# Attention's values product with the values as the stationary side, in three float32r passes, its output already transposed

## What the kernel computes

```python
hcat = jnp.einsum('bsd,de->bse', x, w_in)            # q, k, v of the branches, forget logits, gates
p = jax.nn.softmax(logits, axis=-1)                  # forgetting, block-sparse
o = jnp.einsum('bhqk,bhkd->bhqd', p, v)
# dilated: o and lse per dilation, then
w = jax.nn.softmax(jnp.stack(lses, axis=0), axis=0)
yb = jnp.sum(w[..., None] * jnp.stack(outs, axis=0), axis=0)
merged = sum(gates[:, :, i] * jnp.einsum('bse,ed->bsd', y_i, w_p_i) for i in range(3))
x = layer_norm(alpha * x + jnp.einsum('bsd,de->bse', merged, w_o))
x = layer_norm(alpha * x + swiglu(x))
```

## Time and profile before

| | us |
|---|---|
| runs (3), median | 873.25 (873.02 to 873.25) |
| the profiled execution's own time | 873.52 |
| its span, first to last instruction | 871.7 |
| PE busy | 840.5 (96%) |
| DVE busy | 513.3 (59%) |
| ACT busy | 400.1 (46%) |
| POOL busy | 56.7 (7%) |
| granted TensorE clock, mean | 0.997 |

### The profile page before, as it was taken

The page is one execution under the profiler, slowest core; times in us unless marked ns, Lnnn a source line. Parts: engine busy times, 40 slices in busy tenths (PEclk is TensorE's granted clock), DMA queues, the critical chain, the costliest instruction groups (busy, mean ns, idle before and its releaser), DMA issues.

```text
span 871.7 us, 10732 instructions
## 1 busy us (share of the span) xinstructions
PE 840.5 (96%) x4216; PEld 695.9 (80%) x4216; DVE 513.3 (59%) x728; ACT 400.1 (46%) x536; POOL 56.7 (7%) x86
## 2 busy tenths in 40 slices
PE   3999999999999999999999999999999899999995
PEld 2888888888877888888878889888888688888884
DVE  7565564556796545445685656463778764555436
ACT  3476465543344344444336655554443453344430
POOL 0012331000000000000000324200000000000000
PEclk9999999999999999999999999999999999999998
DMA  9574433457636765664436443435654576656501
GB/s 324 160 257 164 133 119 116 141 181 229 193 104 244 232 194 183 193 203 149 154 108 225 144 159 106 142 103 181 243 177 144 192 246 203 189 183 193 193 0 49
DMA packets 93458, 149.35 MB, mean 171 GB/s; under 512 B 3424, under 2 KB 52832, under 8 KB 93408
## 3 DMA queue, kind: packets, MB, share of 16 engines
q1 hardware_dynamic: 93408, 148.66, 52.5%
HBM read 147.60 MB, written 1.05 MB: 171 GB/s over the span
## 4 chain that ended last, share of the span: by engine, by line
PE 92%; DVE 5%; DMA 1%; ACT 0%; issue 0%; SPq 0%; DVEq 0%
PE bank L1044 82%; PE bank L1059 3%; PE bank L1103 3%; PE bank L1135 2%; DVE w_lo L860 2%; PE bank L1123 1%; PE bank L1069 1%; DMA raw<-in_w_in 1%; DVE stats L977 1%; DVE x L1010 1%; DVE x L974 1%; DVE x L1007 1%; DVE act_lo L865 0%; DVE newton L994 0%; DVE rstd L999 0%
## 5 line engine op out<-in xcount | busy, mean ns | idle before, releaser
L860 DVE TENSOR_TENSOR w_lo<-raw,w_hi 128x2048 fp32r<-128x2048 f32 (+3 forms) x142 | 309.0, 2180 | 91.5 <-ACT w_hi L762 91.0
L1044 PE MATMUL bank<-w_hi,act_hi 128*128 128x512 f32 (+2 forms) x864 | 342.8, 397 | 3.3 <-DVE act_lo L865 3.3
L1044 PE MATMUL bank<-w_hi,act_lo 128*128 128x512 f32 (+2 forms) x864 | 333.3, 386 | 0.0
L1044 PE MATMUL bank<-w_lo,act_hi 128*128 128x512 f32 (+2 forms) x864 | 332.2, 384 | 0.0
L762 ACT CAST w_hi<-raw 128x2048 fp32r<-128x2048 f32 (+3 forms) x142 | 257.2, 1813 | 125.5 <-PE bank L1044 100.4
L1044 PEld LDWEIGHTS bank<-w_hi,act_hi 128*128 128x128 f32 x864 | 163.2, 189 | 33.2 <-DVE act_lo L865 3.7
L1044 PEld LDWEIGHTS bank<-w_hi,act_lo 128*128 128x128 f32 x864 | 162.8, 188 | 33.0
L1044 PEld LDWEIGHTS bank<-w_lo,act_hi 128*128 128x128 f32 x864 | 163.4, 189 | 28.8
L1044 PE MATMUL bank<-w_hi,y_hi 128*128 128x512 f32 x240 | 95.2, 397 | 0.0
L1044 PE MATMUL bank<-w_hi,y_lo 128*128 128x512 f32 x240 | 93.7, 390 | 0.0
L1044 PE MATMUL bank<-w_lo,y_hi 128*128 128x512 f32 x240 | 93.5, 390 | 0.0
(11 more groups left out here) (88 smaller groups left out, 551.3 us busy)
## 6 DMA issues: line engine op xcount, KB each, us to landing
raw<-in_w_in SPq DMA_DIRECT2D x48, 1024.0 KB, 5.2
raw<-in_w_gate SPq DMA_DIRECT2D x44, 512.0 KB, 4.0
raw<-in_w_up SPq DMA_DIRECT2D x44, 512.0 KB, 5.0
raw<-in_w_down SPq DMA_DIRECT2D x22, 1024.0 KB, 4.9
raw<-in_w_o SPq DMA_DIRECT2D x8, 1024.0 KB, 5.2
raw<-in_w_in SPq DMA_DIRECT2D x4, 768.0 KB, 4.4
raw<-in_w_pa SPq DMA_DIRECT2D x4, 768.0 KB, 4.4
raw<-in_w_pc SPq DMA_DIRECT2D x4, 768.0 KB, 4.4
```

The source lines that it names most:

```text
L860: dve.tensor_tensor(weights(w_lo, i, HI_SLOTS), weights(raw, i, RAW_SLOTS), weights(w_hi, i, HI_SLOTS).bitcast(F32), ALU.subtract).then_in ...
L1044: ins = pe.matmul(bank[use[0]][:, 0:width], a, w[:, k, c0:c0 + width], start=start and k == 0 and p == 0, stop=stop and k == nk - 1 and p ...
```

## The change

1. The values are split too: "spread" writes v to `v_hi` (ACT, float32r), DVE makes `v_lo`. There is one buffer for the dilated branch and one that the two other branches share, as now for q and k.
2. A new step "weigh" at half tick k, for unit k-1: DVE takes 1/`denom`. For the forgetting and block-sparse branches DVE also multiplies the probabilities by it in place, one `tensor_scalar` a head. For the dilated branch POOL does that, on the summed probabilities, behind "sum".
3. "turn_p" waits for "weigh", and its result is split: `prob_t_hi` by ACT, `prob_t_lo` by DVE. The buffers hold both tiles of a pair.
4. "values" is done once a pair, after tile 1. The values of the pair (128 columns) are stationary, the transposed probabilities of both heads and tiles move: for key tile 0 512 columns, for key tile 1 256, three passes each. The output has the head's dimension in its rows, and each head's own half of the columns is used (`own_blocks`). ACT and DVE write it straight to `y_hi` and `y_lo`, two operations each on 64 partitions.
5. The transposes of y are gone.

The diff, without the parts that only pass other names or slot lists:

```diff
+Y_SLOTS = [[0, 1, 2], [3, 4], [5, 0, 1]]
...
-                d["pt"] = aux_bank()
+                d["pt"], d["pt_n"] = aux_bank(), count.next("pt")
...
                 stage_of[k]["s2"] = [bank(4), bank(5)]
-                plan.append(("scores2", stage_of[k], g0 + 1))
-            if 0 <= k - 2 < len(units):
+                plan.append(("scores2", stage_of[k]))
+            if 0 <= k - 1 < len(units):
+                plan.append(("weigh", stage_of[k - 1], count.next(("weigh", stage_of[k - 1]["b"] == 1))))
+                stage_of[k - 1]["weigh_n"] = plan[-1][2]
+            if 0 <= k - 2 < len(units) and stage_of[k - 2]["t"] == TT - 1:
                 d = stage_of[k - 2]
                 d["o"] = aux_bank()
-                plan.append(("values", d, g0 + d["b"]))
-                if d["p"] == PAIRS[d["b"]] - 1:
-                    last_y[d["b"], d["t"]] = d["o"]
-                    y_due.append((d["b"], d["t"]))
-
-        y_due = []
-        last_y = {}
+                plan.append(("values", d, count.next("values")))
+                for t in range(TT):
+                    y_turned[d["b"], t] = d["o"]
...
-            for b, t in due:
-                y_turned[b, t] = turn("y", 0, 0, BRANCH_KT[b], t, "y", 3 * ((g0 + b) % 2),
-                                      ("bank", last_y[b, t]))
...
-        values = [sb(f"values{s}", [P, TT, 384]) for s in range(2)]
-        qk_hi = [sb(f"qk_hi{s}", [P, 8, SEQ], F32R) for s in range(2)]
-        qk_lo = [sb(f"qk_lo{s}", [P, 8, SEQ], F32R) for s in range(2)]
+        shapes = [("ac", 384, 6), ("b", 256, 8)]
+        v_hi, v_lo = ([sb(f"v_{part}_{n}", [P, TT, width], F32R) for n, width, _ in shapes] for part in ("hi", "lo"))
+        qk_hi, qk_lo = ([sb(f"qk_{part}_{n}", [P, pairs, SEQ], F32R) for n, _, pairs in shapes]
+                        for part in ("hi", "lo"))
...
-        prob_t = sb("prob_t", [P, 2 * SEQ])
-        y = sb("y", [P, TT, 384])
+        prob_t_hi, prob_t_lo = (sb(f"prob_t_{part}", [P, 3, 2 * P], F32R) for part in ("hi", "lo"))
...
+        def own_blocks(o):
+
+            return [(slice(e * HEAD_DIM, (e + 1) * HEAD_DIM),
+                     o[e * HEAD_DIM:(e + 1) * HEAD_DIM, :].rearrange("p (t e q) -> p t e q", t=TT, e=2)[:, :, e, :])
+                    for e in range(2)]
...
+                elif step[0] == "weigh" and step[1]["b"] == 1:
+                    _, u, n = step
+                    w, pr, s0 = u["w"], both_probs[u["t"]], 2 * (u["u"] % 4)
+                    pool.wait_ge(summed, u["sum_n"])
+                    pool.wait_ge(inverse_done, n)
+                    pool.tensor_tensor(pr[:, :, 0:w], pr[:, :, 0:w],
+                                       rdenom[:, s0:s0 + 2].unsqueeze(2).broadcast_to([P, 2, w]),
+                                       ALU.mult).then_inc(pool_weighed, 1)
...
-                            out = values[(3 * layer + br) % 2][:, t, first:first + width]
+                            out = v_hi[br % 2][:, t, first:first + width]
...
-                    ins.then_inc(drained[b], 1)
+                    ins.then_inc(v_hi_done if v_n else drained[b], 1)
...
-                    act.copy(prob_t[:, 0:2 * u["w"]], bank[b][:, 0:2 * u["w"]]).then_inc(drained[b], 1)
+                    t = u["t"]
+                    act.copy(prob_t_hi[:, t:2 * t + 1, :], group_view(bank[b], t + 1, 2 * P)
+                             ).then_inc(prob_t_hi_done, 1)
+                elif kind == "values":
+                    _, u, _ = step
+                    b, n = u["o"]
+                    act.wait_ge(filled[b], n)
+                    for rows, own_block in own_blocks(bank[b]):
+                        ins = act.copy(hi["y"][rows, Y_SLOTS[u["b"]][u["p"]], :].rearrange("p (t q) -> p t q", t=TT),
+                                       own_block)
+                    ins.then_inc(y_hi_done, 1)
...
+                elif kind == "spread" and step[6]:
+                    _, c, t, (b, n), segs, ev, v_n, _ = step
+                    dve.wait_ge(v_hi_done, v_n)
+                    for what, br, first, col0, width in segs:
+                        if what == "v":
+                            dve.tensor_tensor(v_lo[br % 2][:, t, first:first + width], bank[b][:, col0:col0 + width],
+                                              v_hi[br % 2][:, t, first:first + width].bitcast(F32),
+                                              ALU.subtract).then_inc(drained[b], 1)
...
-                    dve.wait_ge(drained[fb], fn)
+                    dve.wait_ge(v_hi_done, v_n)
...
+                elif kind == "weigh":
+
+                    u = step[1]
+                    s0 = 2 * (u["u"] % 4)
+                    dve.wait_ge(exp_done, 2 * u["u"] + 2)
+                    inverse = dve.reciprocal(rdenom[:, s0:s0 + 2], denom[:, s0:s0 + 2])
+                    if u["b"] == 1:
+                        inverse.then_inc(inverse_done, 1)
+                        continue
+                    link(inverse)
+                    for e in range(2):
+                        pr = prob[u["t"]][e][:, 0:u["w"]]
+                        ins = dve.tensor_scalar(pr, pr, rdenom[:, s0 + e:s0 + e + 1], None, ALU.mult)
+                    ins.then_inc(weighed, 1)
+                elif kind == "turn_p":
+                    u = step[1]
+                    b, n = u["pt"]
+                    t = u["t"]
+                    dve.wait_ge(prob_t_hi_done, u["pt_n"])
+                    dve.tensor_tensor(prob_t_lo[:, t:2 * t + 1, :], group_view(bank[b], t + 1, 2 * P),
+                                      prob_t_hi[:, t:2 * t + 1, :].bitcast(F32),
+                                      ALU.subtract).then_inc(drained[b], 1)
                 elif kind == "values":
-                    u = step[1]
+                    _, u, y_n = step
                     b, n = u["o"]
-                    s0, h0 = 2 * (u["u"] % 4), 2 * u["p"] * HEAD_DIM
-                    dve.wait_ge(filled[b], n)
-                    link(dve.reciprocal(rdenom[:, s0:s0 + 2], denom[:, s0:s0 + 2]))
-                    dve.tensor_tensor(y[:, u["t"], h0:h0 + 2 * HEAD_DIM].rearrange("p (e c) -> p e c", e=2),
-                                      group_view(bank[b], 2, HEAD_DIM),
-                                      rdenom[:, s0:s0 + 2].unsqueeze(2).broadcast_to([P, 2, HEAD_DIM]),
-                                      ALU.mult).then_inc(drained[b], 1)
+                    k = Y_SLOTS[u["b"]][u["p"]]
+                    dve.wait_ge(y_hi_done, y_n)
+                    for rows, own_block in own_blocks(bank[b]):
+                        by_t = [m["y"][rows, k, :].rearrange("p (t q) -> p t q", t=TT) for m in (lo, hi)]
+                        ins = dve.tensor_tensor(by_t[0], own_block, by_t[1].bitcast(F32), ALU.subtract)
+                    ins.then_inc(drained[b], 1)
...
-                    if u["b"] == 1:
-                        pe.wait_ge(summed, u["sum_n"])
-                    else:
-                        pe.wait_ge(exp_done, 2 * u["u"] + 2)
+                    pe.wait_ge(pool_weighed if u["b"] == 1 else weighed, u["weigh_n"])
                     out, done = take(u["pt"])
-                    w = u["w"]
-                    for e in range(2):
-                        for j in range(u["t"] + 1):
-                            ins = pe.transpose(out[:, e * w + j * P:e * w + (j + 1) * P],
-                                               prob[u["t"]][e][:, j * P:(j + 1) * P], ident)
+                    for j in range(u["t"] + 1):
+                        for e in range(2):
+                            c0 = (2 * j + e) * P
+                            ins = pe.transpose(out[:, c0:c0 + P], prob[u["t"]][e][:, j * P:(j + 1) * P], ident)
                     ins.then_inc(done, 1)
...
                 elif kind == "values":
-                    _, u, g = step
+
+                    _, u, _ = step
                     pb_, pn = u["pt"]
                     pe.wait_ge(drained[pb_], pn)
                     out, done = take(u["o"])
-                    w = u["w"]
-                    for e in range(2):
-                        h = 2 * u["p"] + e
-                        for j in range(u["t"] + 1):
-                            ins = pe.matmul(out[:, e * HEAD_DIM:(e + 1) * HEAD_DIM],
-                                            prob_t[:, e * w + j * P:e * w + (j + 1) * P],
-                                            values[g % 2][:, j, h * HEAD_DIM:(h + 1) * HEAD_DIM],
-                                            start=j == 0, stop=j == u["t"])
+                    pair = slice(u["p"] * P, (u["p"] + 1) * P)
+                    for j in range(TT):
+                        cols = slice(j * 2 * P, 4 * P)
+                        for p, (v, pt) in enumerate(((v_hi, prob_t_hi), (v_hi, prob_t_lo), (v_lo, prob_t_hi))):
+                            moving = pt[:, 2 * j:2 + j, :].rearrange("p a q -> p (a q)")
+                            ins = pe.matmul(out[:, cols], v[u["b"] % 2][:, j, pair], moving,
```

(26 more changed lines are left out.)

55 lines of the change are left out of this document (32 added, 23 removed).

## The result

The changed kernel takes 877.34 us (median of 4 runs, 877.08 to 877.74), the kernel before in the same session 873.25 us. The ratio is 1.0045, 95% interval 1.0033 to 1.0058. That is 4.1 us slower. The forecast was 872.4 us, the range ended at 876.2, and "slower" had 0.21. The profiled execution took 877.09 us.

What follows compares the result with a forecast made beforehand. PE was taken to bound the kernel. Per layer, 4.15 us saved against 1.3, 2.0 and 0.4 us of new waits gave -0.45, both layers -0.9, so 872.4 us against 873.25; range 869.4 to 876.2.

Steps and rivals of the forecast that it cites:

- PE's savings: Values product per pair 1.03 instead of 1.35 us, transposes of y gone: 4.15 us a layer, 8.3 together.
- First place: Third scores of unit 7 (dilated first pair, tile 1): PE waits for DVE's reductions behind prob_t_lo; 1.3 us lost a layer.
- Second place: turn_p of unit 7: PE waits for POOL's multiplication, which waits for DVE's reciprocal; 2.0 us lost a layer.
- Third place: Forget gates: two v_lo ahead of f_in on DVE delay cum_row and PE's first scores; 0.4 us lost a layer.
- Elsewhere: Other attention waits stay covered, counted as nothing; unit 11's values product thinly, up to 0.9 us a layer if not.
- DVE's added work: About 15 us more DVE work a layer in attention, most of it falling into DVE's own waits.
- w_lo shuts POOL's multiplication out: Unit 7: DVE's w_lo takes the port first, POOL waits; 875.8 us, 877.6 with unit 11's 0.9 a layer; chance 0.15.
- unit 11's term: Values product of unit 11 waiting for prob_t_lo: up to 0.9 us a layer if its thin cover goes.
- the third rival: Values product: 256-column passes cost as much as long ones, 0.227 us, so 5.4 us comes back; 877.8 us; chance 0.05.
- The first rival: Attention waits are covered better than worked out: 870.5 us, or 865 with no stall and all 8.3 showing; chance 0.30.

Runs made afterwards that it cites:

- Run 2: Changed kernel without DVE's multiplication of the forgetting and block-sparse branches' probabilities by 1/denominator (the reciprocal stays): 876.50 us.
- run 8: Changed kernel with the two v_lo of the third q, k, v product moved behind the forget gates' chain in DVE's queue: 876.16 us.
- run 4: Changed kernel with the values product done half a tick later from unit 7 on, same work: 873.43 us.
- Run 3: Changed kernel with prob_t_lo moved behind the reductions of the same tick in DVE's queue: 874.11 us.
- run 9: Changed kernel with prob_t_lo and dilated reciprocal behind reductions, third product's v_lo behind forget gates, values product half a tick later from unit 7: 866.92 us, again 866.97.
- run 6: Changed kernel with the dilated branch's weighing moved earlier, its reciprocal behind the next unit's reductions: 875.51 us.
- run 5: Changed kernel with the dilated branch's weighing half a tick earlier, right behind the sum and ahead of prob_t_lo: 876.27 us.
- run 7: Changed kernel with DVE instead of POOL weighing the dilated branch's summed probabilities: 876.75 us.
- run 1: Changed kernel without DVE's subtraction that makes prob_t_lo; the buffer holds zeros, PE's passes stay: 870.74 us.

## Why the prediction was wrong

**PE's savings: right within 0.3 us a layer.** The pair costs 1.03 us and y has no transposes. Start to start PE saves about 3.85 us a layer against 4.15 forecast. The difference lies mostly at the first three tile-0 units, whose values product stood next to transposes of q and k: taking it out gave 0.12, 0.41 and 0.39 us there instead of 0.45. PE's busy time fell by 5.7 us where some 8 were forecast. About 2 us of that difference are a low clock in this execution: behind the LayerNorm between the first layer's mixer and FFN (263.8 to 267 us) its product steps took 0.43 us instead of 0.23. Run 2's kernel has the same three groups of waits and no such stretch, and its PE is busy for 832.7 us, 7.8 less than before.

**First place: right in mechanism, at the upper bound in size.** 1.7 us a layer where 1.3 was forecast. It is w_lo, prob_t_lo, reductions, as written. Everything stood later than worked out: the reductions ended at 116.78 and not 115.8, and PE came 0.8 us earlier than before and not 1.4.

**Second place: right.** 1.7 us where 2.0 was forecast. POOL's multiplication took 1.04 us, not the 1.30 of an addition.

**Third place: right in size.** 0.5 and 0.3 us start to start in the two layers, 0.4 forecast; run 8 gives 0.7 of the 0.8 back.

**Elsewhere: this step failed.** "Elsewhere the cover holds ... the values product of unit 11 about 0.2 us after prob_t_lo. That last is thin; if it goes, the price is up to 0.9 us a layer", and the sum took it at nothing. It cost 1.5 us a layer, 3.0 us in all; run 4 confirms it with 3.1. For this place the prediction shows no chain step by step, as it does for the first two. It missed that the displaced reductions move ACT's exponentials, with them w_hi and the w_lo that stands ahead of prob_t_lo. Run 3 shows that link backwards: prob_t_lo moved *behind* the reductions comes earlier at unit 11. Nor had it that turn_p of unit 11 waits for DVE's weighing, 0.17 us a layer.

**DVE's added work** was 17.8 us a layer and not 15. That it was more does not explain the loss: run 9 has nearly all of it.

**The sum.** Set beside each other product step by product step, the two profiled executions give: per layer -3.85, +1.7 +1.7 +1.5, +0.5 or +0.3 at the first scores, and +0.17 at turn_p of unit 11, which is +1.8 and +1.6. Another +0.5 falls outside attention, behind the same LayerNorm, and -0.25 at the start, where the first product came 0.48 us later but the clock rose 1.2 us sooner. Together 3.6 us, as between the spans. The prediction had -0.9 there. Of the 4.5 us between, about 3.0 are unit 11, 0.8 the first place, 0.6 PE's savings, 0.3 turn_p of unit 11, 0.25 what lies outside attention, and the second place gives 0.6 back. The medians are 0.5 us further apart than the profiled executions.

**The rivals.** That w_lo shuts POOL's multiplication out (875.8, 877.6 with unit 11) came nearest in time and did not happen: the multiplication started 0.59 us ahead of w_lo and took 1.04 us. The agreement with 877.6 is chance but for unit 11's term. The lock that the Trainium skill states (page "SBUF — State Buffer", section "Who interferes with whom") fits the rows around it: the addition at 129.33, started into a running w_lo, took 2.26 us instead of 0.73. The 256-column passes ran at 0.11 us, so the third rival is out. The first rival's idea, that the 8 us show once the cover is there, is what run 9 shows with 6.6 of them, but only with another order.

## What to carry to other kernels

When PE is made faster, list for each of its waits what stands ahead on the in-order engine that feeds it, and follow a delay over the next engine too: late reductions gave late exponentials, late w_hi, late w_lo, late prob_t_lo. Work that nobody needs soon, like prob_t_lo, v_lo and 1/denom, goes behind what PE asks for next, and its consumer gets half a tick more. A wait removed alone may be given back in part at the next late producer: of the 3.4 us that run 6's profiled execution won at its two second places, 1.2 went at later scores. And a wait can hide another loss: where the clock fell at the first place, removing the second wait won next to nothing (run 5, first layer).

## What the hardware showed that was not expected

**The clock after a wait.** After the first wait of 1.6 us, PE's granted clock fell in some executions, from the values product that follows, for some 3.5 us. Seven profiled kernels have such a wait, 14 places. The profiled executions of the changed kernel and of runs 2 and 6 have no dip at either layer's first place, that of run 8 has one in both layers, those of runs 4, 5 and 7 in the first layer: 5 of 14. Windows of run 8 (busy us and count of PE, PEld, DVE, ACT and POOL, granted clock, DMA share, GB/s), then one product step of PE's timeline:

```profile
core 0: us, PE busy (x) PEld busy (x) DVE busy (x) ACT busy (x) POOL busy (x), PEclk, DMA share, GB/s
...
118.00:119.00 1.00, 1.00 (x6) 0.87 (x7) 0.97 (x5) 0.46 (x1) 0.00 (x0) 0.93 1.04 403
119.00:120.00 1.00, 1.00 (x5) 1.00 (x4) 0.00 (x0) 1.00 (x3) 0.61 (x1) 0.50 0.12 43
...
122.00:123.00 1.00, 1.00 (x8) 0.80 (x6) 0.97 (x3) 0.00 (x0) 1.00 (x1) 0.86 0.00 0
123.00:124.00 1.00, 1.00 (x19) 1.00 (x18) 1.00 (x1) 0.37 (x1) 0.21 (x1) 1.00 0.00 0
```

```profile
120.03 0.52 PE L1113 MATMUL bank<-w_hi,act_hi 128*128 128x384 f32 x1
```

A clock of 0.50 is 1.2 instead of 2.4 GHz, and a step of 384 columns takes 0.32 instead of 0.18 us. From the values product to the next turn_p PE needs 3.77 us (118.87 to 122.64), in the changed kernel 2.24 (118.51 to 120.75). PE then comes 1.5 us later to turn_p of unit 7 and finds POOL's multiplication done. Where the clock fell, that wait is missing in the trace: in both layers of run 8, in one of runs 4 and 7. So the second place costs about the same either way, once as a wait and once as a slower clock. In run 5 there was no such wait left, and the slower clock cost its time in full. What makes it fall in one execution and not in another stays open. Where the first wait is 0.7 us, in runs 1, 3 and both of run 9, the clock stayed at 1.00 there in all eight places.

**Multiplying on GpSimd is cheaper than adding there.** 128x512 elements times 1/denom (one value per head, broadcast) took 1042 ns, 128x256 616 ns; the addition of two 128x512 tiles took 1287 ns.

**Half the partitions, the same time.** y_lo on 64 partitions and 256 columns took 422 ns on DVE, y_lo on 128 partitions and 256 columns 420 ns. Splitting it by head, as the changed kernel does, costs a second full instruction.
